# Table loads, value products, key requests, down products' banks and the last step of a two-layer backbone kernel

## The reference

```python
qa, ka, va, qb, kb, vb, uc, gz = jnp.split(h @ w_in, IN_SPLITS, axis=-1)
oa = softmax(qa @ ka.T / 8) @ va        # first attention: 8 heads, 2 key heads, keys of context and latent tokens
ob = softmax(window scores + bias, context scores) @ vb     # second attention: 8 heads
oc = real(fft2(uc))                     # Fourier mixing
y = (sig(ga) * (oa @ w_branch[0]) + sig(gb) * (ob @ w_branch[1]) + sig(gf) * (oc @ w_branch[2])) @ w_out
x = layernorm(ALPHA * x + gate * y)
x = layernorm(ALPHA * x + gate2 * ((silu(g) * u) @ w_down))   # g, u = h2 @ w_gu
```

## Time and profile before

| what | value |
|---|---|
| median of 3 runs | 2324.91 us (2324.25 to 2325.17) |
| the profiled execution | 2324.89 us |
| its span in the trace | 2323.1 us |
| PE busy | 2253.0 us (97%), 13050 products |
| DVE busy | 1196.4 us (51%) |
| ACT busy | 940.4 us (40%) |
| POOL busy | 1107.4 us (48%) |
| granted TensorE clock, mean | 0.996 |

### The profile page before, as it was taken

How to read it: one execution, slowest core, us unless ns; L and a number is a source line. 1 busy time by engine, 2 the same in 40 slices (tenths; PEclk the granted TensorE clock), 3 DMA queues, 4 the chain that set the end, 5 groups by cost and what they waited for, 6 DMA issues and landing times.

```text
span 2323.1 us, 34464 instructions
## 1 busy us (share of the span) xinstructions
PE 2253.0 (97%) x13050; PEld 2061.9 (89%) x13050; DVE 1196.4 (51%) x2441; ACT 940.4 (40%) x1878; POOL 1107.4 (48%) x868
## 2 busy tenths in 40 slices
PE   7999999999999999999999999999999999999997
PEld 4899988989999999999998888888889889888887
DVE  6979766527732546654832364656637436112114
ACT  4231466436632651111112364356546547222223
POOL 1434455435534553433534563446545567545555
PEclk9999999999999999999999999999999999999999
DMA  6634200122214445443523453211223255323334
GB/s 267 226 109 145 83 28 28 55 71 75 65 60 136 159 153 192 135 154 112 161 90 118 154 165 121 73 55 37 70 85 96 77 187 190 119 95 102 112 124 169
DMA packets 122388, 270.23 MB, mean 116 GB/s; under 512 B 13956, under 2 KB 14212, under 8 KB 120840
## 3 DMA queue, kind: packets, MB, share of 16 engines
q1 hardware_dynamic: 113312, 245.43, 32.4%
q10 hardware_dynamic: 8936, 22.95, 2.8%
HBM read 254.68 MB, written 10.49 MB: 114 GB/s over the span
## 4 chain that ended last, share of the span: by engine, by line
PE 81%; DVE 10%; ACT 4%; issue 2%; POOL 1%; DMA 1%; ACTq 0%; SPq 0%; DVEq 0%
PE ps L2024 31%; PE ps L2036 12%; PE ps L2026 12%; PE ps L2434 7%; PE ps L2137 7%; PE ps L2404 4%; PE ps L2386 2%; PE ps L2367 2%; DVE pt_lo L1730 1%; PE ps L2213 1%; POOL w_lo L621 1%; DVE ada_unused_gate_up L1260 1%; DVE max_c L1713 1%; DMA raw<-in_stream 1%; DVE ada_unused_merge_c L1260 1%
## 5 line engine op out<-in xcount | busy, mean ns | idle before, releaser
L621 POOL TENSOR_TENSOR w_lo<-raw,w_hi 128x512 fp32r<-128x512 f32 x648 | 887.5, 1392 | 924.8 <-ACT w_hi L699 924.4
L699 ACT ACTIVATE w_hi<-raw 128x512 fp32r<-128x512 f32 x648 | 376.9, 626 | 666.9 <-PE ps L2026 213.0
L2024 PE MATMUL ps<-h_hi,w_lo 128*128 128x512 f32 (+1 forms) x832 | 304.6, 366 | 0.0
L2024 PE MATMUL ps<-h_hi,w_hi 128*128 128x512 f32 (+1 forms) x832 | 303.9, 365 | 0.0
L2024 PE MATMUL ps<-h_lo,w_hi 128*128 128x512 f32 (+1 forms) x832 | 303.9, 365 | 0.0
L633 POOL TENSOR_TENSOR p_sb<-p_sb,row_inv 128x768 f32<-128x768 f32 (+1 forms) x160 | 179.0, 1126 | 205.4 <-DVE row_inv L1723 203.8
L1828 DVE TENSOR_TENSOR ps<-silu_g,ps 128x512 f32<-128x512 f32 (+3 forms) x52 | 36.7, 705 | 354.9 <-PE ps L2024 191.1
L2024 PEld LDWEIGHTS ps<-h_hi,w_hi 128*128 128x128 f32 x832 | 156.2, 188 | 18.6
L2024 PEld LDWEIGHTS ps<-h_hi,w_lo 128*128 128x128 f32 x832 | 156.2, 188 | 18.3
L2024 PEld LDWEIGHTS ps<-h_lo,w_hi 128*128 128x128 f32 x832 | 156.2, 188 | 18.2
L2434 PE MATMUL ps<-h_hi,w_lo 128*128 128x384 f32 (+1 forms) x408 | 147.8, 362 | 1.0 <-ACT gates_a L1024 0.7
(11 more groups left out here) (246 smaller groups left out, 5461.4 us busy)
## 6 DMA issues: line engine op xcount, KB each, us to landing
raw<-in_stream SPq DMA_DIRECT2D x648, 256.0 KB, 2.9
ada_raw_gate_up<-in_w_ada SPq DMA_DIRECT2D x48, 512.0 KB, 3.5
ada_raw_tokens_a<-in_w_ada SPq DMA_DIRECT2D x16, 512.0 KB, 5.3
ada_raw_merge_c<-in_w_ada SPq DMA_DIRECT2D x16, 512.0 KB, 3.6
bias_sb<-in_bias ACTq DMA_DIRECT2D x32, 256.0 KB, 2.7
scratch<-xr ACTq DMA_DIRECT2D x16, 512.0 KB, 4.7
xr<-scratch SPq DMA_DIRECT2D x14, 512.0 KB, 4.9
first_raw<-in_w_first SPq DMA_DIRECT2D x5, 1024.0 KB, 14.2
```

The source lines that it names most:

```text
L621: nc.gpsimd.tensor_tensor(w_lo[:, u % 2, cols], raw[:, u % 2, cols], w_hi[:, u % 2, cols].bitcast(F32), ALU.subtract).then_inc(S("lo_made" ...
L699: nc.scalar.activation(w_hi[:, s, cols], raw[:, s, cols], ACT.Copy).then_inc(S("hi_made"), 1)
L2024: last = nc.tensor.matmul(bank(0), tile, x[:, k, 0:split], start=start, stop=stop)
```

## The change

1. `load_table(ACT.Exp)` moves from `merge_c` and `values` to the start of each attention, and the calls for Sigmoid in the next to last slots go; loads for Sigmoid stand where the merges' first Sigmoid is (L956, L964 of before).
2. `attend` makes all products with `pt_hi` of its groups first, each group waiting for `hi_out`, and then those with `pt_lo`, waiting for `lo_out`. Products and their number are the same.
3. In DVE's `late_slot` the rests of keys and queries come before both halves of `pt_lo`, not between them.
4. The key copies are requested by ACT, right behind the copy that they read, no more by SP.
5. `down` uses four bank pairs in turn (`DOWN_BANKS = 4`) where it used two; PE may be four units ahead of DVE's sums.
6. In the last group of the last bridge each tile's mean follows its sum at once, and the last tile's shift and store come in two halves of 512 columns.

```diff
...
 PRODUCT_BANKS = 3
+DOWN_BANKS = 4
 MERGE_BANKS = ((7, 2, 0, 4, 2, 0, 4, 6), (6, 2, 0, 4, 2, 0, 4, 6))
...
+def last_rows(ph, g):
+
+    return ph.kind == "bridge" and ph.part == 1 and ph.layer == DEPTH - 1 and g == len(ph.groups) - 1
+
+
 def ada_beside(ph):
...
-            def key_copies(ph, u):
-
-                if ph.kind == "values" and u == ph.unit + 4:
-                    c, filled = 0, at(ph, "fill_out") + 1
-                elif ph.kind == "attention" and ph.part and u - ph.unit in (5, 7, 9):
-                    f = u - ph.unit - 4
-                    c, filled = f // 2 + 1, at(ph, "fill_out") + passes_to(ph, f + 1)
-                else:
-                    return
-                sp.wait_ge(S("fill_out"), filled)
-                for x in range(2):
-                    n = 2 * (c % 2) + x
-                    sp.dma_start(k_hh[1][HD * (1 - x):HD * (2 - x), n, :].bitcast(F32), k_hh[1][HD * x:HD * x + HD, n, :].bitcast(F32)
-                                 ).then_inc(S("k_dup"), 16)
-
             def rows_of(ph, t):
...
                         beside(ph, u)
-                    else:
-                        key_copies(ph, u)
                 if u >= 2:
...
                     dst = out[t, :, :] if ends(ph) else scratch[2 * ph.layer + ph.part + 1, t, :, :]
+                    if last_rows(ph, g) and i == len(ph.groups[g]) - 1:
+                        act.dma_start(out[t, :, 0:LAT], xr[:, t, 0:LAT]).then_inc(S("stored"), 16)
+                        act.wait_ge(S("shifted"), at(ph, "shifted") + len(ph.groups[0]) * g + i + 2)
+                        act.dma_start(out[t, :, LAT:D], xr[:, t, LAT:D]).then_inc(S("stored"), 16)
+                        continue
                     act.dma_start(dst, xr[:, t, :]).then_inc(S("stored"), 16)
...
+            def key_copies(c, filled):
+
+                act.wait_ge(S("fill_out"), filled)
+                for x in range(2):
+                    n = 2 * (c % 2) + x
+                    act.dma_start(k_hh[1][HD * (1 - x):HD * (2 - x), n, :].bitcast(F32), k_hh[1][HD * x:HD * x + HD, n, :].bitcast(F32)).then_inc(S("k_dup"), 16)
+
             def value_hi(ph, t):
...
                 act.wait_ge(S("merged"), at(ph, "merged"))
-                load_table(ACT.Exp)
                 for j in range(2):
...
                 unit_done(ph.unit, 0, lambda: key_parts(0, qk_bank(0, 1), 0, TOK))
+                key_copies(0, at(ph, "fill_out") + 1)
                 unit_done(ph.unit + 1, 1, lambda: query_parts(0, qk_bank(0, 0), 0, ph.width))
...
                             act.wait_ge(S("ada_used"), PRIME - ADA_FIRST + ADA_WINDOWS[ph.kind][1])
-                        load_table(ACT.Exp)
                         for name in start_pieces(nxt):
...
                         fill_out(f, len(fill_passes(ph, f)) - 1)
+                        if f < 6 and f % 2:
+                            key_copies(f // 2 + 1, at(ph, "fill_out") + passes_to(ph, f + 1))
                     if early is not None:
...
                         probs(n + 1, 1)
-                    if n == count - 2:
-                        load_table(ACT.Sigmoid)
                     for g in groups[:2]:
...
+                load_table(ACT.Exp)
                 act.wait_ge(S("merged"), at(ph, "merged"))
...
                         probs(n + 1, 1)
-                    if n == count - 2:
-                        load_table(ACT.Sigmoid)
                     for g in groups[2:]:
...
                         split(ph.unit + f + 2, f % 2)
+                        if branch == 1 and f < 6 and f % 2:
+                            key_copies(f // 2 + 1, at(ph, "fill_out") + passes_to(ph, f + 1))
                     h, j = divmod(n, pairs)
...
                                                    accum_out=sum_s[:, 0, t:t + 1]).then_inc(S("added"), 1)
-                    if i:
+                    if last_rows(ph, g):
+                        tile_mean(i)
+                    elif i:
                         tile_mean(i - 1)
-                tile_mean(len(tiles) - 1)
+                if not last_rows(ph, g):
+                    tile_mean(len(tiles) - 1)
...
                     scaled = span(ROWS_BANK[i % 2], D) if stays(ph, g, i) else xn[:, slot_of(ph, g, i), :]
+                    if last_rows(ph, g) and i == n - 1:
+                        for half in range(2):
+                            cols = slice(LAT * half, LAT * (half + 1))
+                            nc.vector.scalar_tensor_tensor(xr[:, t, cols], scaled[:, cols], inv_s[:, t:t + 1], ln_rows[:, 1, cols],
+                                                           ALU.mult, ALU.add).then_inc(S("shifted"), 1)
+                        return
                     nc.vector.scalar_tensor_tensor(xr[:, t, :], scaled, inv_s[:, t:t + 1],
...
                 def tile_mean(i):
+                    if ends(ph):
+                        return
                     dve.wait_ge(S("shifted"), at(ph, "shifted") + base + i + 1)
-                    if not ends(ph):
-                        mean(ph, 1, tiles[i])
+                    mean(ph, 1, tiles[i])
...
                         invert(n + 1, 1)
-                    turned_lo(n, 0)
                     if late is not None:
...
                         fill_rest(early, 0)
-                    for g in groups[1:]:
+                    for g in groups:
                         turned_lo(n, g)
...
-                def pair(i, ada):
-                    for s in range(2):
-                        if s and ada:
-                            ada_three("gate_up", beside[0] // ADA_SLOTS + i)
-                        n = 2 * i + s
+                def several(i, ada):
+                    for s in range(DOWN_BANKS):
+                        n = DOWN_BANKS * i + s
+                        if s % 2 and ada:
+                            ada_three("gate_up", (beside[0] + ADA_SLOTS * (n // 2)) // ADA_SLOTS)
                         dve.wait_ge(S("unit_done"), ph.unit + n + 1)
...
                 if beside:
-                    for i in range(KD // 2):
-                        pair(i, True)
+                    for i in range(KD // DOWN_BANKS):
+                        several(i, True)
                 else:
-                    with dve.Fori(0, KD // 2) as i:
-                        pair(i, False)
+                    with dve.Fori(0, KD // DOWN_BANKS) as i:
+                        several(i, False)
...
                     groups = turn_groups(branch, j)
+
+                    def product_of(g, kt, pt, rows=slice(0, P), start=False):
+
+                        users = [t for t in ORDER[branch][j] if kt in key_tiles(branch, t)]
+                        first = min(users, key=lambda t: t % 2)
+                        w, out_col = P * len(users), 2 * P * (n % 2) + P * (first % 2)
+                        a = 512 * g + turn_col(branch, j, g, kt, first)
+                        v = v_a[:, kt, h // 4, :] if branch == 0 else v_b[:, h // 2, kt, h % 2, :]
+                        return nc.tensor.matmul(ps[rows, OUT_BANK[branch], out_col:out_col + w], v[:, 0:rows.stop - rows.start],
+                                                pt[branch][:, a:a + w], start=start, stop=pt is pt_lo and g == len(groups) - 1,
+                                                skip_group_check=True)
+
                     for g in some:
...
                             wait(pe, "folded", at(ph, "folded") + n)
+                        pe.wait_ge(S("hi_out"), at(ph, "hi_out") + turns["p", n, g] + 1)
+                        for kt in groups[g]:
+                            product_of(g, kt, pt_hi, start=g == 0 and kt == groups[0][0])
+                    for g in some:
                         pe.wait_ge(S("lo_out"), at(ph, "lo_out") + turns["p", n, g] + 1)
                         for x, kt in enumerate(groups[g]):
-                            v = v_a[:, kt, h // 4, :] if branch == 0 else v_b[:, h // 2, kt, h % 2, :]
-                            users = [t for t in ORDER[branch][j] if kt in key_tiles(branch, t)]
-                            w, side = P * len(users), P * (min(users, key=lambda t: t % 2) % 2)
-                            out_col = 2 * P * (n % 2) + side
-                            a = 512 * g + turn_col(branch, j, g, kt, min(users, key=lambda t: t % 2))
-                            for pt in (pt_lo, pt_hi):
-                                last = nc.tensor.matmul(ps[:, OUT_BANK[branch], out_col:out_col + w], v, pt[branch][:, a:a + w],
-                                                        start=g == 0 and x == 0 and pt is pt_lo,
-                                                        stop=g == len(groups) - 1 and x == len(groups[g]) - 1 and pt is pt_hi,
-                                                        skip_group_check=True)
+                            last = product_of(g, kt, pt_lo)
                     if len(groups) - 1 in some:
...
-                pe.wait_ge(S("summed"), at(ph, "summed") - 1)
```

(15 more changed lines are left out.)

## The result

The changed kernel takes 2301.06 us (median of 4 runs, 2299.45 to 2302.15) where the kernel before took 2325.04 beside it. The ratio is 0.9893, 95% interval 0.9876 to 0.9911, so 1.1% faster. Taken from the 2324.91 that the forecast started from, the ratio gives 2300.2 us, just outside the range's low end of 2301. The forecast gain was 17.6 us; the traces are 24.0 apart (2323.1 and 2299.1). The changed kernel was run twice more, beside other executions of the kernel before: medians 2303.01 (0.9904) and 2301.3 (0.9899). So a kernel's median moves by up to 2 us from one set of runs to the next, and what follows reads parts of about 1 us from the traces, place by place, and not from medians.

A forecast was written before the change was run, and what follows sets the result against it. PE, busy 97% of the time, bounds the kernel, so only its waits, about 70 us, can move. Terms -1.6 - 4.1 - 1.2 - 7.3 - 2.3 - 0 - 0 - 1.1 = -17.6 from 2324.89 give 2307.3 us; range 2301 to 2316.

The forecast's parts named there:

- Table loads: Loads moved off PE's way at layer 1's first scores and the attentions' ends: -5.7 us, added loads counted 0.
- the -1.65: End of layer 0's first attention: of 1.98 us lost, load's 1.40 delay of `pt_hi` goes and high products start early.
- the time near 2302: Four load removals on PE's way worth up to 1.26 us more each by the skill page; given no weight.
- High products first in the first attentions: Layer 0's first attention: high products fill up to 0.24 us in each of seven waits; -1.2 (0 to -1.7).
- the factor of eight tenths: Layer 0's second attention: share of 9.1 us of waits expected to go, giving -7.3 (-4 to -9.1).
- the 0.16 added for each: Correction in us added to each wait's bracket removed whole, as a bracket understates a loss; 1.9 for layer 0's 12.
- One worked slot: Query slot at 553.51 in layer 0's second attention, where 0.8 of 1.06 us was expected to go.
- off PE's path: Key requests on ACT: a pair of at most 1.1 us fits idle time or delays `p_sb` by 0.4; 0.
- Rival 3: ACT holds at its key requests until landing, 4.9 us a pair on `pt_hi`'s path: +29, 2336 us; chance 0.03.
- weights are no earlier: Last down products, layer 0: PE would wait for weights as long as for DVE's sums; 0 (0 to -3.3).
- the sign of being right: Last down products still with 3 us of PE waits, now named after weights (`w_lo` or `w_hi`), not `acc`.
- The end: Last step: first square about 1.0 us earlier gives -0.6, last shift in halves -0.5; -1.1 (0 to -1.5).

The follow-up runs named there:

- the second trace of before: The kernel before, run once more with nothing changed: 2326.04 us (1.0004), its profile 2321.77 us.
- the kernel with weights first: Changed kernel with SP requesting the next unit's weights ahead of the conditioning requests, beside down products only: 2299.93 us (0.9894), again 2299.14 (0.9887).

## Why the prediction was right and where it was too small

- **Direction and main mechanism: right.** PE's count is unchanged, and what went are waits and the time at half clock behind one of them. The order of terms held: the second attention of layer 0 first, the loads next.
- **What failed are terms of the sum.** The traces are 6.4 us further apart than the 17.6 forecast. Of this, 2.2 lie in layer 0's first attention (1.5 of them the clock, which had no term), 1.85 in the down products (put at 0), 1.0 in layer 0's second attention, 0.5 in layer 1's first, 0.4 at the end and 1.0 in unchanged work; 0.6 went the other way.
- **Table loads, -5.7 forecast, -4.8 measured.** Right at layer 1's first scores (1.54 for 1.5); 0.2 to 0.4 too much at each end of an attention. The new places cost nothing that a row shows. A load put back moved PE by 0.77 to 1.54. Part of the -1.65 was for high products that start early, which is in the next point's measurement. The 2.66 us a switch of the Trainium skill, page "ScalarE: Activation LUTs", section "What ACT_TABLE_LOAD costs", was not seen. That the time near 2302 that the prediction worked out from it lies close to the measured one is chance: the loads put back cost 4.8 in all, not the 5.7 of the sum and 5 more.
- **High products first in the first attentions: too small.** -1.2 was forecast for layer 0 and nothing for layer 1; -2.0 and -0.7 were measured (1.3 and 0.7 in layer 0, ahead of 400 us and behind). The waits for `p_sb` took back what the prediction said (0.5 grew to 1.3), but the products at the attention's end gained 0.7 as well, and layer 1 was left out.
- **Second attention of layer 0: the factor of eight tenths was wrong.** All twelve waits went: 8.3 of the 9.1 that were counted, where the surplus is the 0.16 added for each, closer to 0.09. One worked slot was taken for all. In layer 1 undoing both orders costs 2.35 and DVE's alone 2.2, for -2.3 forecast, but that agreement is luck: with the key requests on SP the three waits are worth 2.86, and the changed kernel has 1.81 of it, as the key requests take back 1.05.
- **Key requests: 0 and "off PE's path" failed.** The price of a pair was bounded by 1.1, though the earlier trace rows has a single request of 1.265; one pair took 2.0, and its 0.9 reached PE through `p_sb` and DVE's order. Rival 3 needed six pairs of 3.8 to make the kernel slower; the slow pair took 2.0 and the others 1.1, and ACT's next activation began 0.1 behind them.
- **Four bank pairs, 0 forecast, 0.7 to 1.85 measured.** The step "weights are no earlier" held in the main at the first wait (1.7 gained, 1.35 given back). It failed at the second, of which "the same pattern" was said: there the weights were in time. So the sign of being right, 3 us of waits named after weights, did not come: one of 1.1 did.
- **The end, -1.1 forecast, -1.4 measured.** The mechanism was right; the second mean held up nothing.
- **Left out altogether: the clock.** The prediction read the wait before 421.08 and not the granted clock behind it, where about 1.5 us lay. It could have been seen in the trace of before, but not counted on: the second trace of before lacks it.

The range's low end was near the sum with all its gains full, 2301.5. The measured time lies beyond it although the largest of these did not come in full (banks 1.85 of 3.3, second attention of layer 0 8.3 of 9.1), because of what the sum did not have: the clock, layer 1's high products, and 1.0 of unchanged work that differs as much between executions of one kernel. By how little it lies beyond is luck of the runs: the two later ratios give 2302.6 and 2301.4, inside the range.

## What to carry to other kernels

Behind each long wait of PE read the granted clock too: a wait of 1.8 us cost up to 1.6 more, in one execution and not in the next. Take a second trace of the unchanged kernel before sharing out a gain by place: here two of them differ by 3.1 us. Where an order or an engine's requests are moved, look at the slowest issue of that kind in the trace, not the middle one, before calling it hidden. Once a bank or buffer wait is gone, look for the next one in the request order of another queue; here it was worth as much as the banks.

## What was unexpected of the hardware

- Half clock (1.2 GHz) for 3.4 us followed waits of 1.77, 1.82 and 2.03 us, and not in each execution of one kernel; the loss was 0.9 to 1.6 us.
- A conditioning row on DVE (128 x 1024, bfloat16 out) took 1.22 us alone and 2.12 to 2.35 beside POOL's `w_lo`; a start 0.01 us behind or 0.26 ahead of `w_lo` decided which.
- One DMA request on ACT or SP took 1.35 to 1.83 us where the middle one takes 0.54, in the same place in ten of thirteen traces of the changed kernel and its variants.
- Two executions of the changed kernel differ by 1.7 us in the first 40 us and by 1.2 between 240 and 258 us. Those of the kernel with weights first differ by 4.2 in layer 1 between 1826 and 2006 us, of which half clock is some 1.5; the rest is not explained.
